# A hybrid transformer kernel: the long-convolution filters built from joined weights on VectorE, and the spectrum's products on VectorE over 1024 columns

## The reference

```python
def hyena_filters(n, w1, b1, w2, b2, w3, freq):
    ...
    h = (h @ w3.astype(f32)).reshape(n, HY_ORDER, 2, HY_CH)
    deltas = jnp.abs(jnp.linspace(HY_MIN_DECAY, HY_MAX_DECAY, HY_CH, dtype=f32))
    h = h * jnp.exp(-t[:, None, None, None] * deltas)
    kern = jnp.concatenate([h[:, :, 0], jnp.zeros((1, HY_ORDER, HY_CH), f32), jnp.flip(h[1:, :, 1], axis=0)], axis=0)
    kern = kern * lax.rsqrt(jnp.sum(kern * kern, axis=0, keepdims=True) + EPS)
    return jnp.fft.rfft(kern, axis=0)

def hyena(u, conv_w, kf, bias):
    v, x1, x2 = jnp.split(dwconv(u, conv_w), 3, axis=-1)
    z = v
    for o, gate in enumerate((x1, x2)):
        z = gate * (fft_long_conv(z, kf[:, o]) + z * bias[o])
    return z
```

## Time and profile before

| what | value |
|---|---|
| median of three runs | 2585.8 us (2580.39 to 2587.72) |
| the profiled execution's own time | 2582.52 us |
| its span, first to last instruction | 2580.7 us |
| PE busy, share of the span | 2352.9 us, 91% |
| DVE, ACT, POOL busy | 34%, 21%, 12% |
| mean granted TensorE clock | 0.961 |
| stage `attention_and_filters` | 1787 to 1940 us from the span's start |
| stage `convolutions` | 1940 to 2041 us |

### The profile page before, as it was taken

How to read it: one execution, slowest core, us unless ns; L and a number is a source line. 1 busy time by engine, 2 the same in 40 slices (tenths; PEclk the granted TensorE clock), 3 DMA queues, 4 the chain that set the end, 5 groups by cost and what they waited for, 6 DMA issues and landing times. The chain is left out here.

```text
span 2580.7 us, 37602 instructions
## 1 busy us (share of the span) xinstructions
PE 2352.9 (91%) x16466; PEld 1615.4 (63%) x16466; DVE 879.0 (34%) x1653; ACT 544.5 (21%) x1266; POOL 318.5 (12%) x363
## 2 busy tenths in 40 slices
PE   4999899979966999999999999898887799999998
PEld 1556655558855755555558999544543584444798
DVE  2125722277641422222220003333666532222111
ACT  2103622321202311111110012111551131111111
POOL 1000100047630000000001000000563200000000
PEclk9999899989987999999999999998898899999999
DMA  8341011000021212121205557411000222222354
GB/s 315 131 163 34 1 33 33 1 2 4 4 82 52 66 33 66 33 66 33 66 25 153 162 165 209 138 49 45 1 1 17 65 66 86 77 66 87 90 148 133
DMA packets 190534, 193.46 MB, mean 75 GB/s; under 512 B 4691, under 2 KB 174370, under 8 KB 190178
## 3 DMA queue, kind: packets, MB, share of 16 engines
q1 hardware_dynamic: 177506, 145.53, 18.6%
q0 software_dynamic: 11776, 42.27, 4.5%
q10 hardware_dynamic: 1088, 3.26, 0.4%
HBM read 188.94 MB, written 2.10 MB: 74 GB/s over the span
## 5 line engine op out<-in xcount | busy, mean ns | idle before, releaser
L1442 PE MATMUL banks<-mem 128*128 128x512 f32 x1312 | 618.1, 591 | 0.0
L1776 PE MATMUL banks<-mem 128*128 128x128 f32 x3520 | 403.5, 276 | 11.4 <-PEq L1365 9.9
L1776 PEld LDWEIGHTS banks<-mem 128*128 128x128 f32 x3520 | 398.8, 193 | 21.4 <-issue 20.1
L1442 PEld LDWEIGHTS banks<-mem 128*128 128x128 f32 x1312 | 247.8, 189 | 171.9 <-issue 153.2
L362 DVE SCALAR_TENSOR_TENSOR mem<-banks,mem 128x511 f32<-128x511 f32 (+1 forms) x168 | 106.1, 660 | 702.8 <-ACT mem L1513 325.3
L1445 PEld LDWEIGHTS banks<-mem 128*128 128x128 f32 x672 | 127.1, 189 | 161.9 <-issue 161.9
L1445 PE MATMUL banks<-mem 128*128 128x256 f32 x672 | 200.1, 378 | 0.0
L1861 PE MATMUL banks<-mem 128*128 128x512 f32 x400 | 190.8, 608 | 6.0 <-issue 6.0
L1511 ACT ACTIVATE mem<-banks,mem 128x512 f32<-128x512 f32 x88 | 60.7, 689 | 626.6 <-PE banks L1445 373.5
L1387 PE MATMUL banks<-mem 128*128 128x256 f32 x640 | 143.3, 384 | 14.5 <-PEq L616 11.1
L921 PE MATMUL banks<-mem 64*64 64x64 f32 x3840 | 127.8, 220 | 18.5 <-DVE mem L1197 11.4
(11 more groups left out here) (330 smaller groups left out, 2693.9 us busy)
## 6 DMA issues: line engine op xcount, KB each, us to landing
mem<-in_ffn_w_up SPq DMA_DIRECT2D x44, 1024.0 KB, 5.5
mem<-in_ffn_w_down SPq DMA_DIRECT2D x64, 704.0 KB, 6.5
mem<-in_w_mod POOLq DMA_DIRECT2D x40, 1024.0 KB, 7.4
mem<-in_ab_w_in SPq DMA_DIRECT2D x14, 1024.0 KB, 5.3
mem<-in_w_mod SPq DMA_DIRECT2D x8, 1024.0 KB, 14.1
mem<-in_cd_w_in SPq DMA_DIRECT2D x8, 1024.0 KB, 5.3
mem<-in_ab_w_out SPq DMA_DIRECT2D x4, 1024.0 KB, 9.2
mem<-in_cd_w_out SPq DMA_DIRECT2D x4, 1024.0 KB, 9.1
```

The costliest lines, as they stand in the source:

```text
L1442: last = nc.tensor.matmul(c.ps[:, bank, :], w[:, k, :], ht[:, k, 0:N_X], start=k == 0, stop=k == KT - 1)
L1776: last = c.nc.tensor.matmul(c.ps[:, n % self.n_banks, 0:128], hidden[:, k, t * 128:(t + 1) * 128], w, start=k == 0, stop=k == FT - 1)
```

## The change

It changes who does the filter work, and how the products are cut.

- Before the first lag product, GpSimd makes joined weights once (`join_sides`): for either order the sum and the difference of the two sides' weights, on 64 partitions, into space of the weight ring, and a small tile `first` that corrects lag 0, where the second side doesn't count. So the lag products give sum and difference directly; the step of lag block 0 has a second matmul for the correction. TensorE's first product waits for GpSimd's eighth instruction of `join_sides` (`joined`) where it waited for the loads.
- VectorE multiplies each lag product with the decay straight out of PSUM into `lags` (`Filters.weigh`). ScalarE's copies of them are gone. Its squares read `lags`, and GpSimd only adds them up.
- In unfold steps ScalarE copies the even half alone; VectorE reads the odd half from PSUM and forms difference and sum (`unfold`), behind the two maxima of the step.
- In `convolutions` GpSimd's part of the product is gone. VectorE does six products and sums over 1024 columns (both mirror halves at once, 128x2x512) and four sums of 512, where it did six and five of 512.

```diff
--- before.py
+++ after.py
...
+        self.joined = c.ring[0:HEAD, 4096:6144].rearrange("p (o s n) -> p o s n", o=2, s=2)
+        self.first = c.ring[0:HEAD, 6144:6400].rearrange("p (s n) -> p s n", s=2)
...
+    def lags_before(self, n):
+        return 4 * (n // 8) + min(n % 8, 4)
...
+    def join_sides(self, pool):
+        hy, g = self.hy, self.c.nc.gpsimd
+        pool.wait_ge(self.came, self.LOADED)
+        side = lambda order, s: hy.w3[:, (2 * order + s) * 512:(2 * order + s) * 512 + 512]
+        for sign in range(2):
+            g.memset(hy.first[:, sign], 0.0).then_inc(self.joined, 1)
+        pool.wait_ge(self.joined, 2)
+        g.tensor_scalar(hy.first[:, 0, 0:1], hy.h2[:, 0:1], -1.0, None, ALU.mult).then_inc(self.joined, 1)
+        g.tensor_copy(hy.first[:, 1, 0:1], hy.h2[:, 0:1]).then_inc(self.joined, 1)
+        for order in range(2):
+            g.tensor_tensor(hy.joined[:, order, 0], side(order, 0), side(order, 1), ALU.add).then_inc(self.joined, 1)
+            g.tensor_tensor(hy.joined[:, order, 1], side(order, 0), side(order, 1), ALU.subtract).then_inc(self.joined, 1)
+
+    JOINED = 8
...
-            pe.wait_ge(self.came, self.LOADED)
+            pe.wait_ge(self.joined, self.JOINED)
         if n:
-            pe.wait_ge(self.kept, 2 * (n - 1) + part + 1)
+            if self.is_lag(n - 1):
+                pe.wait_ge(self.ready, 2 * self.lags_before(n - 1) + part + 1)
+            elif part:
+                pe.wait_ge(self.unfolded, 2 * self.unfolds_before(n - 1) + 2)
+            else:
+                pe.wait_ge(self.even_kept, self.unfolds_before(n - 1) + 1)
         if lag:
-            t, col = n % 8, (order * 2 + part) * 512
-            last = c.nc.tensor.matmul(out, hy.h2[:, t * 128:(t + 1) * 128], hy.w3[:, col:col + 512], start=True, stop=True)
+            t = n % 8
+            last = c.nc.tensor.matmul(out, hy.h2[:, t * 128:(t + 1) * 128], hy.joined[:, order, part], start=True, stop=t > 0)
+            if t == 0:
+                other = hy.w3[:, (2 * order + 1) * 512:(2 * order + 1) * 512 + 512]
+                last = c.nc.tensor.matmul(out, hy.first[:, part], other, start=False, stop=True)
...
+    def weigh(self, dve, n, part):
         hy = self.hy
+        if self.is_lag(n):
+            order, t = n // 8, n % 8
+            if n == 0 and part == 0:
+                dve.wait_ge(self.came, self.LOADED)
+            dve.wait_ge(self.product, 2 * n + part + 1)
+            self.c.nc.vector.tensor_tensor(hy.lags[:, part, t, :], self.c.ps[:, self.banks[part], :], hy.decay[:, t, :],
+                                           ALU.mult).then_inc(self.ready, 1)
+
+    def keep_even(self, act, n):
+        c, hy = self.c, self.hy
+        if not self.is_lag(n):
+            f, s = (n % 8 - 4) // 2, n % 2
+            act.wait_ge(self.product, 2 * n + 1)
+            c.nc.scalar.activation(hy.kern[n // 8][:, s, f], c.ps[:, self.banks[0], :], ACT.Copy).then_inc(self.even_kept, 1)
+
+    def unfold(self, dve, n):
+        v, hy, order = self.c.nc.vector, self.hy, n // 8
+        if not self.is_lag(n):
+            f, s = (n % 8 - 4) // 2, n % 2
+            total, mirrored, odd = hy.kern[order][:, s, f], hy.kern[order][:, s, 2 + f], self.c.ps[:, self.banks[1], :]
+            dve.wait_ge(self.product, 2 * n + 2)
+            dve.wait_ge(self.even_kept, self.unfolds_before(n) + 1)
+            v.tensor_tensor(mirrored, *((odd, total) if s else (total, odd)), ALU.subtract).then_inc(self.unfolded, 1)
+            dve.wait_ge(self.unfolded, 2 * self.unfolds_before(n) + 1)
+            v.tensor_tensor(total, total, odd, ALU.add).then_inc(self.unfolded, 1)
...
-                act.wait_ge(self.decayed, 2 * lags + part + 1)
+                act.wait_ge(self.ready, 2 * lags + part + 1)
+                self.c.nc.scalar.activation(self.hy.lag_sq[part], self.hy.lags[:, part, n % 8, :], ACT.Square,
+                                            scale=math.sqrt(0.5)).then_inc(self.squared, 1)
...
-        pe.wait_ge(self.kept, 2 * self.STEPS)
+        pe.wait_ge(self.even_kept, 8)
+        pe.wait_ge(self.unfolded, 16)
...
@@ -2927,9 +2939,8 @@
 
             for i in range(n_pairs + 2):
                 if 0 <= i - 2:
-                    filters.keep(act, i - 2)
-                if 0 <= i - 3:
-                    filters.square(act, i - 3)
+                    filters.keep_even(act, i - 2)
+                    filters.square(act, i - 2)
...
+            filters.join_sides(pool)
...
@@ -2983,7 +2995,15 @@
                 if i < n_pairs:
                     maximum(2 * i)
                     maximum(2 * i + 1)
+                if 0 <= i - 2:
+                    filters.unfold(dve, i - 2)
+                if 0 <= i - 1 < n_pairs:
+                    filters.weigh(dve, i - 1, 0)
+                if i < n_pairs:
                     weigh(2 * i)
+                if 0 <= i - 1 < n_pairs:
+                    filters.weigh(dve, i - 1, 1)
+                if i < n_pairs:
                     weigh(2 * i + 1)
...
                 tt(hy.vb[:, t, :], hy.v[:, t, :], hy.bias0, ALU.mult).then_inc(weighted, 1)
-            for order in range(2):
...
-                    pool.wait_ge(unfolded, 2 * g + 2)
-                    if g:
-                        pool.wait_ge(spec_done, g)
-                    tt(one_s, z(0, 0), kern(1, 0), ALU.mult)
-                    link(tt(part_s, z(1, 0), kern(0, 0), ALU.mult))
-                    tt(one_s, one_s, part_s, ALU.add)
-                    tt(other_s, z(0, 1), kern(1, 1), ALU.mult)
-                    tt(other_part_s, z(1, 1), kern(0, 1), ALU.mult).then_inc(spec_s, 1)
...
@@ -3133,7 +3137,7 @@
...
             def multiply(order, f):
                 g = 2 * order + f
-                kern = lambda s, mirror: hy.kern[order][:, s, 2 * mirror + f, :]
+                kern = lambda s: hy.kern[order][:, s, f::2, :]
...
                 dve.wait_ge(unfolded, 2 * g + 2)
-                for mirror, total in enumerate((one, other)):
-                    v.tensor_tensor(total, z(0, mirror), kern(0, mirror), ALU.mult)
-                    link(v.tensor_tensor(part, z(1, mirror), kern(1, mirror), ALU.mult))
-                    link(v.tensor_tensor(total, total, part, ALU.subtract))
+                v.tensor_tensor(sums, hy.z[0], kern(0), ALU.mult)
+                link(v.tensor_tensor(parts, hy.z[1], kern(1), ALU.mult))
+                link(v.tensor_tensor(sums, sums, parts, ALU.subtract))
+                v.tensor_tensor(sums_s, hy.z[0], kern(1), ALU.mult)
+                link(v.tensor_tensor(parts, hy.z[1], kern(0), ALU.mult))
+                last = v.tensor_tensor(sums_s, sums_s, parts, ALU.add)
+                last.then_inc(spec_c, 1)
+                dve.wait_ge(spec_c, g + 1)
                 if order and f == 0:
                     dve.wait_ge(inverse, 4)
-                v.tensor_tensor(hy.spec[:, 0, f, :], one, other, ALU.add)
-                v.tensor_tensor(hy.spec[:, 0, 2 + f, :], one, other, ALU.subtract).then_inc(spec_c, 1)
-                dve.wait_ge(spec_s, g + 1)
-                link(v.tensor_tensor(other_s, other_s, other_part_s, ALU.add))
-                v.tensor_tensor(hy.spec[:, 1, f, :], one_s, other_s, ALU.subtract)
-                v.tensor_tensor(hy.spec[:, 1, 2 + f, :], one_s, other_s, ALU.add).then_inc(spec_done, 1)
+                v.tensor_tensor(hy.spec[:, 0, f, :], sums[:, 0], sums[:, 1], ALU.add)
+                v.tensor_tensor(hy.spec[:, 0, 2 + f, :], sums[:, 0], sums[:, 1], ALU.subtract)
+                v.tensor_tensor(hy.spec[:, 1, f, :], sums_s[:, 0], sums_s[:, 1], ALU.subtract)
+                v.tensor_tensor(hy.spec[:, 1, 2 + f, :], sums_s[:, 0], sums_s[:, 1], ALU.add).then_inc(spec_done, 1)
...
```

More of the change, by code:

```diff
@@ L2718, in multiply @@
         last.then_inc(self.product, 1)
-    def place(self, n, part):
+    def weigh(self, dve, n, part):
         hy = self.hy
[L2724 to L2736, removed]
-            c.nc.scalar.activation(self.place(n, part), c.ps[:, self.banks[part], :], ACT.Copy, scale=scale)\
-                .then_inc(self.kept, 1)
@@ L2740, in after @@
-    def after(self, eng, n):
-        lags, lag = self.lag_step(n)
-        if lag:
-            eng.wait_ge(self.ready, 2 * (lags + 1))
-            eng.wait_ge(self.squared, 2 * (lags + 1))
-        else:
-            eng.wait_ge(self.unfolded, 2 * (4 * (n // 8) + n % 8 - 4 + 1))
+        if self.is_lag(n):
[5 more added lines that the diff above has]
+                                           ALU.mult).then_inc(self.ready, 1)
@@ L2760, in weigh, with add @@
-    def weigh(self, pool, n):
+                self.c.nc.scalar.activation(self.hy.lag_sq[part], self.hy.lags[:, part, n % 8, :], ACT.Square,
+                                            scale=math.sqrt(0.5)).then_inc(self.squared, 1)
+    def add(self, pool, n):
         hy, g = self.hy, self.c.nc.gpsimd
-        lags, lag = self.lag_step(n)
-        order, t = n // 8, n % 8
-        if n == 0:
```

(19 more changed lines are left out.)

53 lines of the change are left out of this document (21 added, 32 removed).

## The result

The changed kernel takes 2569.19 us, median of five runs (2563.94 to 2573.27); the kernel before, in the same comparison, 2580.99. The ratio is 0.9946, 95% interval 0.9927 to 0.9966: faster by 12 us between the medians, 14 by the ratio. The forecast was 2568, from a sum of -14.7. The profiled execution has a span of 2570.0 us, 10.7 less than the earlier trace rows.

The account below looks back on a forecast made before the run. TensorE, busy 2352.9 of 2580.7 us, was taken as the bound, with movable waits in two stages. Terms summed to -14.7 from the profiled 2582.5, giving 2567.8 (2568) us; range 2557 to 2578, forecast holding for 2562 to 2573.

Parts of the forecast that it names:

- the load is at an end of its bounds: Stated sign of a wrong prediction: GpSimd's library load before the first lag product costs nearly 0 or 14.2 us.
- the clock falls in a lag step: Stated sign of a wrong prediction: TensorE's clock falls in the filter stage's lag steps, expected at 1.00.
- start, to step 2: Before the first lag product: GpSimd's join delays it by 3.3 us, two more matmuls add 2.1; +5.4 us.
- library load: GpSimd's library load ahead of the first lag product: between 0 and 14.2 us, middle taken, +7 us.
- steps 2 to 4: Lag steps of `attention_and_filters`: VectorE, the longest queue, takes 7.5 us a step, 22.5 where 24.3 were; -1.9 us.
- step 5: First unfold step of one order: TensorE's wait for GpSimd's last difference goes, 7.6 us where 15.3 were; -7.7 us.
- steps 6 to 12: Unfold steps 6 to 8 lengthen to 8.2 us as TensorE awaits VectorE's unfolding; 9 to 12 give -0.2; together +2.6 us.
- step 13: First unfold step of the other order, with 512 keys: 5.5 us where 15.9 were; -10.4 us.
- `convolutions`: Four VectorE chains before inverse transforms take 9.8 us where 12.3 were, -9.9, and -1 from the clock; -10.9 us.
- Rival 1: GpSimd's library load costs nothing, since the same library is in place; sum -21.7, 2561 us; chance 0.17.
- rival 3: GpSimd's sums of squares hold VectorE in every lag step; +10 us, 2578 us; chance 0.13.
- rival 4: TensorE falls to 1.2 GHz in the lag steps once gaps reach about 3 us; +18 to +19, 2587 us; chance 0.07.

Follow-up runs that it names:

- e3: The changed kernel with its one-column operation as a difference of two tiles, needing no library load; join 5.8 us, single run 2561.87 us.
- e7: The changed kernel without the second matmul for lag 0 in steps n = 0 and 8; first maximum of step 1 to step 2 took 10.7 us.
- e10: The changed kernel with VectorE's six products of 1024 columns as twelve of 512; ratio 0.9937.
- e12: The changed kernel with VectorE's copy of the values right behind maxima and whole unfolding, not at the step's end; 2560.95 us, ratio 0.9910.
- e4: The changed kernel with VectorE's whole unfolding ahead of the two maxima of its step; ratio 0.9934.
- e6: The changed kernel with the unfolding's difference ahead of the maxima, its sum behind them, then the copy of the values; 2560.46 us, ratio 0.9904.
- e11: The changed kernel again, unaltered, for a second trace; 2574.65 us, ratio 0.9950 against the kernel before.
- e8: The kernel before without GpSimd's five operations of each `multiply` and the waits for them; the `convolutions` stage took 82.9 us instead of 101.5.
- e9: The changed kernel with split unfolding, early copy, and TensorE's first product waiting for order 0's joined weights alone; 2558.19 us, ratio 0.9898.

## Why the prediction was right, point by point

The time was right within 1.2 us, and so was the direction. The size was forecast as -14.7 and is -10.7 in the profile, -11.8 between the medians; the rest was made up by the base, 2582.5, which lies 1.5 above the median of the kernel before in this comparison. And the sum came that near by luck: a term of +7 that was not there stood against others that were too favourable by 11 us on balance. By the signs that the prediction gave for itself it failed: the load is at an end of its bounds, and the clock falls in a lag step.

| term | predicted | measured in the profile after |
|---|---|---|
| start, to step 2 | +5.4 | +8.3 |
| library load | +7 | 0.1 at most |
| steps 2 to 4 | -1.9 | -0.1 |
| step 5 | -7.7 | -7.9 |
| steps 6 to 12 | +2.6 | +1.7 |
| step 13 | -10.4 | -7.0 |
| step 14 to the norm | +1.2 | +1.2 |
| `convolutions` | -10.9 | -8.6 |
| behind it | 0 | +1.6 |
| sum | -14.7 | -10.7 |

- *Library load.* The step that failed: "I take the middle, +7". Rival 1 was right on this, though its time, 2561, was not; the gap is 0.09 us in the changed kernel and 0.08 without the load (e3). What the Trainium skill, "GPSIMD Engine Reference", section 2.1 Instruction dispatch, gives for the first call to a freshly loaded kernel, about 6 us, isn't seen here; the trace has an earlier load of this kind at 227.3 us, so that the library was already in place is likely, but no run tests it. The 14.2 us of the earlier trace rows were something else; no run shows what.
- *Start.* The join took 5.8 us as worked out. "The first lag step has two more matmuls ... +2.1" counted one pair; there are two, 1.91 us and 2 x 1.06 at 1.2 GHz, and e7 gives 3.8 for both. The other 1.2 us is the stage's own later start: its first maximum of step 1 is at 1802.04 after, 1800.83 before. Over the traces of this study that mark lies between 1799 and 1810.
- *Steps 2 to 4 and step 13.* The reading of the earlier trace rows was off: the 23 us hold VectorE's work of nearly three steps, not of 2.3. From the first maximum of step 2 to that of step 5 VectorE is busy 18.1 us before, 17.6 after and 17.4 in e10, so 6.0 and 5.9 us a step and not 7.7 and 7.5. The difference of 0.2 a step is as forecast, but VectorE's work isn't what sets these steps. Its single operations do cost what was taken: the decay takes 0.69, also at 1831.58 beside a sum of GpSimd's that runs from 1830.77 to 1832.04, and only single weighings met GpSimd's sums (1.25 us for one of 0.49), so rival 3 did not come. The rule of the Trainium skill, "SBUF — State Buffer", section "Who interferes with whom", has a condition that the prediction leaves out: an operation with at most one SBUF input doesn't contend when it is outside VectorE's two-port modes, which a `tensor_scalar` can enter. The weighing is one, with one SBUF input, and is the one held; whether it ran in such a mode no run here shows. With the clock at its upper level steps 2 to 4 take 19.9 us (e10), better than the forecast 22.5, which came from that reading. But rival 4 came in part: idle times of 1.8 us, not 3, went before a fall at step 3 and at step 13, and the falls cost 4.3 and 1.7 us (8.9 against e10's 7.2). "It decides once gaps reach about 3 us" was too high a bound, and no gap alone decides: 1.86 us was followed by either level. The 5.5 of step 13 also left out that TensorE waits for the copy at the end of VectorE's step (1.86 us at 1902.9); e12 with the early copy has 6.4.
- *Step 5.* Right: with GpSimd out of the chain the wait is gone, both in time and in the list of waits.
- *Steps 6 to 8.* Right: TensorE waits for line 2776, five times up to 0.7 us, and a step takes 8.15 (predicted 8.2; three of them at 0.9 over 7.3 make +2.7, not the +2.8 written). e4 adds that the loop has a second one of 7.96 right behind it, and e6 that both go when the unfolding is split, at 7.4.
- *`convolutions`.* The chain came out as worked out, 9.8 us, and the idle times lost 10.3 in sum (predicted 9.9). The step that failed is the clock's "-1": the matmuls of the stage took 1.7 us longer in this trace instead (10.15 us for a transform that took 8.98, 6.37 for the first group that took 5.55), and the stage took 92.9 us in the second trace too (e11). The rule of the Trainium skill, "SBUF — State Buffer", section "Who interferes with whom", agrees with these traces: operations with two inputs from SBUF beside a GpSimd that reads SBUF take 1.63 to 1.76 us before, and 0.69 in e8 without it.
- *Behind.* The stages after the two take 1.6 us longer in the one trace than in the other; nothing in them changed.

## What to carry to other kernels

Work that is given to GpSimd to relieve VectorE is not free for VectorE: here five GpSimd operations held six VectorE ones by 5.0 us, more than the 3.3 that VectorE needs for their work, and taking them back made the chain shorter. When work moves to an in-order engine, ask for each of its instructions which other engine waits for it, and put that one first: moving one copy of 0.29 us from the end of VectorE's step to its middle gave about 0.4%, as much as either part of the change. And a sum that comes out right is no proof of its terms: read each off the trace after.

## What the runs showed of the hardware

- GpSimd's load of its library in the middle of the program, behind an earlier one, took no time that the trace or the run without it shows (0.09 against 0.08 us).
- A VectorE operation of 512 float32 columns with two SBUF inputs took 0.69 us alone and 1.63 to 1.76 beside GpSimd's operations of the same kind (before and e8).
- TensorE's clock fell after idle times of 1.76 and 1.86 us in some executions; after 1.86 it stayed up in another with the same instructions in the stage (e10). It also fell after 1.12 us in e12, and stayed up after 1.13 in e9. Steps 2 and 3 together took 17.2 or 12.9 us. That is nearly half of the spread of 9 us among the changed kernel's first five runs; that the clock makes the whole spread is not shown, but the granted clock over a whole run went with its time (0.967 in the run of 2563.94, 0.960 in that of 2573.27).
